# Two decoder layers on one core: FF2's units of seven products, block transposes by way of HBM, and sums behind the remainders

## The reference, cut to what matters

```python
def conv_gated_ffn(h, w_up, conv_w, conv_b, w_down):      # h 256x2048, w_up 2048x11264, w_down 5632x2048
    u = h @ w_up
    up_ = jnp.pad(u, ((0, 0), (1, 1), (0, 0)))
    u = up_[:, :-2] * conv_w[0] + up_[:, 1:-1] * conv_w[1] + up_[:, 2:] * conv_w[2] + conv_b
    gate, val = jnp.split(u, 2, axis=-1)
    return (jax.nn.silu(gate) * val) @ w_down
```

## Time and profile before

| what | value |
|---|---|
| median of 3 runs | 2124.67 us (2124.34 to 2125.66) |
| profiled execution, its own time | 2125.52 us |
| its span | 2123.4 us |
| PE busy | 2108.5 us, 99% |
| DVE busy | 1738.8 us, 82% |
| ACT busy | 1194.7 us, 56% |
| POOL busy | 80.4 us, 4% |
| HBM read | 395.80 MB, 190 GB/s over the span |

### The profile page before, as it was taken

How to read it: one execution, slowest core, us unless ns; L and a number is a source line. 1 busy time by engine, 2 the same in 40 slices (tenths; PEclk the granted TensorE clock), 3 DMA queues, 4 the chain that set the end, 5 groups by cost and what they waited for, 6 DMA issues and landing times.

```text
span 2123.4 us, 28090 instructions
## 1 busy us (share of the span) xinstructions
PE 2108.5 (99%) x9682; PEld 1753.0 (83%) x9682; DVE 1738.8 (82%) x2498; ACT 1194.7 (56%) x1562; POOL 80.4 (4%) x114
## 2 busy tenths in 40 slices
PE   9999999999999999999999999999999999999999
PEld 7897888888888888888889878888888888888887
DVE  5889977888888887979766557569999999999787
ACT  6556675555555545545466446556666666665454
POOL 1000000001000100000000042000000000000000
PEclk9999999999999999999999999999999999999999
DMA  7665355677767767566556544466666666656665
GB/s 225 197 181 169 111 181 155 214 231 231 224 208 227 237 213 242 191 215 199 173 164 173 169 115 152 148 184 187 194 191 185 199 188 194 190 184 199 210 198 178
DMA packets 219710, 404.81 MB, mean 191 GB/s; under 512 B 14335, under 2 KB 58953, under 8 KB 219371
## 3 DMA queue, kind: packets, MB, share of 16 engines
q1 hardware_dynamic: 215755, 391.13, 59.5%
q0 software_dynamic: 3696, 11.54, 1.7%
q10 hardware_dynamic: 176, 1.06, 0.1%
HBM read 395.80 MB, written 7.86 MB: 190 GB/s over the span
## 4 chain that ended last, share of the span: by engine, by line
PE 82%; DVE 11%; issue 4%; ACT 2%; DMA 0%; DVEq 0%; ACTq 0%; POOL 0%; POOLq 0%
PE ps L679 20%; PE ps L681 20%; PE ps L680 20%; PE ps L985 6%; PE ps L986 6%; PE ps L987 6%; DVE w_lo L2075 3%; DVE gate_T L2128 2%; DVE val_T L2128 1%; PE ps L717 1%; ACT w_hi L1398 1%; DVE stage L2941 1%; DVE stage L2949 1%; DVE cv L2187 1%; PE ps L741 0%
## 5 line engine op out<-in xcount | busy, mean ns | idle before, releaser
L2075 DVE TENSOR_TENSOR w_lo<-raw,w_hi 128x1024 fp32r<-128x1024 f32 (+2 forms) x701 | 837.7, 1209 | 210.5 <-ACT w_hi L1398 204.0
L1398 ACT ACTIVATE w_hi<-raw 128x1024 fp32r<-128x1024 f32 (+2 forms) x701 | 724.6, 1045 | 459.2 <-PE ps L681 348.3
L679 PE MATMUL ps<-w_hi,hT_hi 128*128 128x512 f32 (+2 forms) x1792 | 699.8, 390 | 3.0 <-DVE w_lo L2075 2.3
L681 PE MATMUL ps<-w_hi,hT_lo 128*128 128x512 f32 (+2 forms) x1792 | 690.6, 385 | 0.0
L680 PE MATMUL ps<-w_lo,hT_hi 128*128 128x512 f32 (+2 forms) x1792 | 690.3, 385 | 0.0
L679 PEld LDWEIGHTS ps<-w_hi,hT_hi 128*128 128x128 f32 x1792 | 336.6, 188 | 72.7 <-DVE w_lo L2075 6.9
L681 PEld LDWEIGHTS ps<-w_hi,hT_lo 128*128 128x128 f32 x1792 | 336.4, 188 | 63.2
L680 PEld LDWEIGHTS ps<-w_lo,hT_hi 128*128 128x128 f32 x1792 | 336.8, 188 | 59.8
L679 PE MATMUL ps<-w_hi,aT_hi 128*128 128x512 f32 x480 | 187.1, 390 | 0.8 <-DVE w_lo L2075 0.8
L681 PE MATMUL ps<-w_hi,aT_lo 128*128 128x512 f32 x480 | 186.8, 389 | 0.0
L680 PE MATMUL ps<-w_lo,aT_hi 128*128 128x512 f32 x480 | 186.7, 389 | 0.0
(11 more groups left out here) (391 smaller groups left out, 2324.0 us busy)
## 6 DMA issues: line engine op xcount, KB each, us to landing
raw<-in_w_up SPq DMA_DIRECT2D x264, 512.0 KB, 4.2
raw<-in_w_down SPq DMA_DIRECT2D x176, 512.0 KB, 4.7
raw<-in_w_gate SPq DMA_DIRECT2D x88, 512.0 KB, 3.8
raw<-in_w_in SPq DMA_DIRECT2D x80, 464.0 KB, 3.7
raw<-in_w_out SPq DMA_DIRECT2D x64, 512.0 KB, 4.0
raw<-in_w_in SPq DMA_DIRECT2D x64, 256.0 KB, 3.2
raw<-in_w_in SPq DMA_DIRECT2D x24, 448.0 KB, 3.5
turn_rows<-stage POOLq DMA_DIRECT2D x11, 512.0 KB, 5.0
```

What stands on the lines that cost most here:

```text
L679: pe.matmul(o, xh, wh, start=first, stop=False)
L681: mm = pe.matmul(o, xl, wh, start=False, stop=last)
L1398: act.activation(w_hi[:, s, :kc, :width], raw[:, s, :kc, :width], ACT.Copy).then_inc(hi_ready, 1)
L2075: dve.tensor_tensor(w_lo[:, s, :kc, :width], raw[:, s, :kc, :width], w_hi[:, s, :kc, :width].bitcast(F32), ALU.subtract).then_inc(lo_ready, 1)
```

## The change

In each of the ten loop turns of FF2 the last gate tile (pair 7) and the value tile of the same pair stand next to each other and form one unit of seven: `up_seven` on TensorE, `up_combine`, `up_combine_rest`, `up_extra` and `up_value_add` on VectorE, `up_unit_hi` on ScalarE. Its combinations `up_comb` lie where `x_sb` lies, so `x_sb` (2 MB) is stored to `x_rows` in HBM before the loop and loaded back behind it, both on GpSimd's queue.

The 16 strip transposes of each half are replaced by two block transposes, a store to HBM and four strip loads; ScalarE reads the strips (`strips2`) into `half_T` before `center2`. The gate's rows have a buffer of their own (`gate_rows`), the value's rows lie in `stage[:, 2]`. The taps of the gate stand ahead of the unit in the turn, those of the value in its last third. One turn stands ahead of the loop, written out. In the groups of w_down, `sums` stands behind the remainder of the pair's first tile instead of ahead of it, and the product of the last block is split at pair 6 of group 2.

```diff
+UP_ORDER = [(0, i) for i in range(8)] + [(1, 7)] + [(1, i) for i in range(7)]
+UP_UNIT = 7
+UNITS1 = len(FF1_UNIT) * (FB - 1)
...
+                if name == "x3":
+                    pool.dma_start(x_rows, x_sb[:].rearrange("p t n -> p (t n)")).then_inc(x_saved, 16)
+
+                    def up_strips(j, half, again):
+
+                        pool.wait_ge(turned, FB + 2 * j - 1 + half)
+                        pool.sem_inc(pool_seen)
+                        pool.dma_start(turn_rows[half], turn_out).then_inc(turn_saved, 16)
+                        pool.wait_ge(turn_saved, 16 * (FB + 2 * j - 1 + half))
+                        pool.sem_inc(pool_seen)
+                        if again and half == 0:
+                            pool.wait_ge(aT_ready, j - 1)
+                            pool.sem_inc(pool_seen)
+                        strips_back(half, stage[:, 1 + half].rearrange("p c s -> p (c s)"))
+
+                    up_strips(1, 0, False)
+                    up_strips(1, 1, False)
+                    with pool.Fori(2, FB + 1) as j:
+                        up_strips(j, 0, True)
+                        up_strips(j, 1, True)
+                    pool.wait_ge(ff_value, 2 * (FB - 1))
+                    pool.dma_start(x_sb[:].rearrange("p t n -> p (t n)"), x_rows).then_inc(x_back, 16)
...
+            def up_seven(j):
...
+                pe.wait_ge(lo_ready, c + 1 + 16 * j)
+                three(ps[:, 4, :], a11, b11, True, True)
+                three(ps[:, 0, :], a12, b21, False, True).then_inc(tile_used, 1)
+                pe.wait_ge(gemm_free[1], G_FF2 + j)
+                pe.wait_ge(lo_ready, c + 2 + 16 * j)
+                three(ps[:, 2, :], sums[3], b22, True, False).then_inc(tile_used, 1)
+                pe.wait_ge(ff_split, 2 * UNITS1 + 2 * j - 1)
+                three(ps[:, 7, :], sums[0], comb[0], True, True)
+                three(ps[:, 6, :], sums[1], comb[1], True, True).then_inc(ff_used, 1)
+                pe.wait_ge(ff_split, 2 * UNITS1 + 2 * j)
+                three(ps[:, 5, :], sums[2], comb[2], True, True)
+                three(ps[:, 1, :], a22, comb[3], False, True).then_inc(ff_used, 1)
...
+                for n in range(UP_UNIT):
+                    gemm_tile(T_FF2 + n, 16 * j, H, 2 * n, pair(0), n == 0, False)
+                up_seven(j)
+                for n in range(UP_UNIT + 2, 16):
+                    up_value_tile(n, j)
...
+            def strips2(j, half):
+
+                act.wait_ge(turn_back, 64 * (FB + 2 * j + 1 + half))
+                act.activation(by_strip(half_T[:].rearrange("p c s -> p (c s)")),
+                               stage[:, 1 + half].rearrange("p c s -> p (c s)").rearrange("p (i m a) -> p i m a", i=4, a=32),
+                               ACT.Copy).then_inc(value_turned if half else gate_turned, 1)
...
+            def up_unit_hi(j):
+
+                c = T_FF2 + UP_UNIT + 1
+                act.wait_ge(raw_landed[c % RING], landed(c, 16 * j))
+                act.wait_ge(tile_used, c - RING + 1 + 16 * j)
+                act.activation(w_hi[:, c % RING, 1, :], raw[:, c % RING, 1, :], ACT.Copy).then_inc(hi_ready, 1)
+                for i in range(2):
+                    act.wait_ge(ff_ready, 2 * UNITS1 + 2 * j - 1 + i)
+                    act.activation(up_comb_hi[:, 2 * i:2 * i + 2, :], up_comb[:, 2 * i:2 * i + 2, :], ACT.Copy).then_inc(ff_hi, 1)
+
+            def up_turn(j, after):
+
+                hi_tiles(T_FF2, 16 * j, 0, 4)
+                copy2(j - 1, 1, after)
+                hi_tiles(T_FF2, 16 * j, 4, 5)
+                strips2(j - 1, 0)
+                center2(j - 1, 0)
+                hi_tiles(T_FF2, 16 * j, 5, 7)
+                silu2(j - 1)
+                hi_tiles(T_FF2, 16 * j, 7, 8)
+                up_unit_hi(j)
+                hi_tiles(T_FF2, 16 * j, 9, 11)
+                act.wait_ge(ff_used, 2 * UNITS1 + 2 * j)
+                act.activation(up_comb[:, 0, :], ps[:, 4, :], ACT.Copy).then_inc(ff_copied, 1)
+                hi_tiles(T_FF2, 16 * j, 11, 13)
+                copy2(j, 0, True)
+                hi_tiles(T_FF2, 16 * j, 13, 14)
+                strips2(j - 1, 1)
+                center2(j - 1, 1)
+                hi_tiles(T_FF2, 16 * j, 14, 16)
+                hidden_hi(j - 1)
...
-                    if b == 0 and (q, p) in SUM_AT:
-                        sums(SUM_AT[q, p])
                     if b == 0 and p in SEVEN[q]:
                         combine(q, p)
                     if b == 1 and p in SEVEN[q]:
                         second_chunk_lo(c)
                     else:
                         split_lo(c, 0)
+                    if b == 0 and (q, p) in SUM_AT:
+                        sums(SUM_AT[q, p])
                     if (q, p, b) == (0, 6, 1):
                         turn_lo(FB - 1)
+                    if (q, p, b) == (2, 6, 1):
+                        hidden_lo(FB - 1)
...
+            def up_blocks(half):
+
+                for t in range(TOK):
+                    out = turn_out.rearrange("p (q c t a) -> p t c q a", q=4, c=4, t=TOK)[:, t]
+                    ins = dve.transpose(out, up_rows[half][:, t, :].rearrange("p (c q b) -> p c q b", c=4, q=4))
+                ins.then_inc(turned, 1)
...
+            def up_combine(j):
...
+                dve.tensor_tensor(t1, raw[:, sb_, 0, :], raw[:, sa, 0, :], ALU.subtract)
+                dve.tensor_tensor(t3, raw[:, sb_, 1, :], raw[:, sb_, 0, :], ALU.subtract).then_inc(ff_ready, 1)
+                dve.wait_ge(ff_ready, 2 * UNITS1 + 2 * j - 1)
+                dve.tensor_tensor(t2, raw[:, sb_, 1, :], t1, ALU.subtract).then_inc(ff_step, 1)
+                dve.wait_ge(ff_step, 4 * (FB - 1) + 3 * j - 2)
+                dve.tensor_tensor(t4, raw[:, sa, 1, :], t2, ALU.subtract).then_inc(ff_ready, 1)
...
+            def up_extra(j, part):
+
+                u1, u2, u3, u4 = (up_comb[:, i, :] for i in range(4))
+                if part == 0:
+                    dve.wait_ge(ff_copied, FB - 1 + j)
+                    dve.tensor_tensor(u2, ps[:, 5, :], u1, ALU.add).then_inc(ff_step, 1)
+                    dve.tensor_tensor(ps[:, 0, :], ps[:, 0, :], u1, ALU.add)
+                    dve.wait_ge(ff_step, 4 * (FB - 1) + 3 * j - 1)
+                    dve.tensor_tensor(u4, ps[:, 7, :], u2, ALU.add)
+                    dve.tensor_tensor(u3, ps[:, 6, :], u2, ALU.add).then_inc(ff_step, 1)
+                else:
+                    dve.wait_ge(ff_step, 4 * (FB - 1) + 3 * j)
+                    dve.tensor_tensor(u2, ps[:, 7, :], u3, ALU.add)
+                    dve.tensor_tensor(ps[:, 1, :], ps[:, 1, :], u3, ALU.add).then_inc(ff_added, 1)
...
+            def up_value_add(j):
+
+                dve.wait_ge(tile_used, T_FF2 + 16 + 16 * j)
+                dve.wait_ge(ff_added, FB - 1 + j)
+                dve.tensor_tensor(ps[:, 2, :], ps[:, 2, :], up_comb[:, 3, :], ALU.add)
+                dve.tensor_tensor(ps[:, 3, :], ps[:, 3, :], up_comb[:, 1, :], ALU.add).then_inc(ff_value, 1)
+                dve.wait_ge(ff_value, FB - 1 + j)
+
+            def up_turn(j, after):
+
+                lo_tiles(T_FF2, 16 * j, 0, 3)
+                if after:
+                    up_value_add(j - 1)
+                lo_tiles(T_FF2, 16 * j, 3, 5)
+                dve.wait_ge(gemm_free[1], G_FF2 + j)
+                dve.wait_ge(turn_saved, 16 * (FB + 2 * j - 1))
+                up_blocks(1)
+                lo_tiles(T_FF2, 16 * j, 5, 6)
+                taps2(j - 1, 0, (0,))
+                lo_tiles(T_FF2, 16 * j, 6, 7)
+                taps2(j - 1, 0, (1,))
+                up_combine(j)
                 lo_tiles(T_FF2, 16 * j, 7, 8)
-                taps2(j - 1, 1)
+                up_combine_rest(j)
+                lo_tiles(T_FF2, 16 * j, 9, 11)
+                up_extra(j, 0)
+                lo_tiles(T_FF2, 16 * j, 11, 12)
+                up_extra(j, 1)
+                lo_tiles(T_FF2, 16 * j, 12, 13)
+                dve.wait_ge(gemm_free[0], G_FF2 + 1 + j)
+                dve.wait_ge(turn_saved, 16 * (FB + 2 * j))
+                up_blocks(0)
+                lo_tiles(T_FF2, 16 * j, 13, 14)
+                taps2(j - 1, 1, (0,))
+                lo_tiles(T_FF2, 16 * j, 14, 15)
+                taps2(j - 1, 1, (1,))
                 product2(j - 1)
-                lo_tiles(T_FF2, 16 * j, 8, 12)
+                lo_tiles(T_FF2, 16 * j, 15, 16)
                 hidden_lo(j - 1)
-                dve.wait_ge(gemm_free[0], G_FF2 + 1 + j)
-                dve.wait_ge(aT_ready, j)
-                dve.wait_ge(ct_free, 2 * j)
-                for n in range(4):
-                    lo_tiles(T_FF2, 16 * j, 12 + n, 13 + n)
-                    ins = turn_strips(gate_T[:], raw_s, 4 * n, 4 * n + 4)
-                ins.then_inc(gate_turned, 1)
+
+            dve.wait_ge(x_saved, 16)
+            up_turn(1, False)
+            with dve.Fori(2, FB) as j:
+                up_turn(j, True)
```

(4 more changed lines are left out.)

168 lines of the change are left out of this document (101 added, 67 removed).

## The result

| | before | after |
|---|---|---|
| median, us | 2124.59 (4 runs) | 2149.55 (4 runs, 2145.68 to 2152.00) |
| profiled execution, its span | 2125.52, 2123.4 | 2145.68, 2143.9 |
| matmuls, whole page | 9682 | 9652 |

The ratio is 1.0115, interval 1.0097 to 1.0133: 25 us slower. I had forecast 2126.9 us and 2139 as the upper end. Between the profiled executions it is 20.2 us, and only those can be compared row by row. The four runs of after rose one after the other while their mean granted clock went from 1.000 to 0.998.

The account below looks back on a forecast made before the run. TensorE's matmul count was taken as the bound. On the profiled 2125.52 us, -6.8 - 3.0 + 10 x 1.0 + 10 x 0.2 + 0 + 0 = +2.2 gave 2127.7, median 2126.9 us; 8-in-10 range 2116 to 2139.

Parts of the forecast that it names:

- The products: FF2 loop: one unit in each of ten turns removes 3 matmuls per turn, saving 6.8 us.
- VectorE's lighter load: FF2 turn: VectorE's work falls by 2.3 us net, to about 39 of 42.85 us, so by sum it fits.
- The old waits: FF2 loop: the existing stalls, 0.30 us a turn, go as VectorE gets lighter, saving 3.0 us.
- The chain behind the unit: FF2, unit to last tile: TensorE waits for the last remainder, 1.0 us in each of ten turns (0.5 to 1.3).
- From there to the next unit: FF2, last tile to next unit: 0.3 us margin against 0.5 us transfer delay, 0.2 us stall a turn (0 to 1.5).
- Rival C: FF2, strips behind tile 4: gate rows return late, stalling the unit; +12 us at 6.5 us landing, 2139 us; chance 0.20.
- The range: Whole kernel: the main case's own range, 2121 to 2133 us, said to come from both bounds of the chain.
- x_sb to HBM and back: Around the FF2 loop: storing 2 MB and loading it in w_down costs 0, at most 3 us each way.
- Sums behind remainders: w_down, third group: the gap at pair 15 closes but returns at pair 16; counted 0, between -1.3 and 0.

Follow-up runs that it names:

- e3: The changed kernel, with VectorE splitting the last tile's remainder ahead of the previous block's value product; 2156.34 us, ratio 1.0145 to the kernel before.
- e6: e2 with the last tile's remainder ahead of the value's product and the hidden split behind the next turn's first tile; 2136.44 us, ratio 1.0044.
- e10: e7 with last block's product and split later in w_down, value add right behind the first tile's remainder, value rows copied one tile earlier; 2124.46 us.
- e2: The changed kernel, with gate strips returning into gate_rows in blocks 0 to 9, not waiting for the hidden split; 2134.61 us, ratio 1.0043.
- e9: The changed kernel with the two handovers moved as in e6, but gate strips still returning into stage[:, 1] behind the hidden split; 2166.79 us.
- e1: The changed kernel, with the 2 MB return of x_sb sent as eight 256 KB pieces, one after every third tile; 2146.44 us, ratio 1.0101.
- e5: The changed kernel without the unit of seven products in FF2: pair 7 multiplied plainly, transposes through HBM kept; 2126.07 us, ratio 0.9996.
- e7: e6 plus e1's spaced return of x_sb, and the last block's gate strips returning into up_comb_hi without waiting for the hidden split; 2132.62 us.
- e11: e10, with tiles 10 and 11 of w_down's second group split ahead of the last block's value strips; 2122.70 us, ratio 0.9983.
- e4: The kernel before, with only w_down's sums moved behind the tile's first remainder; 2124.81 us, ratio 0.9992.

## Why the prediction was wrong

- *The products*, -6.8 us, and VectorE's lighter load: right (30 matmuls fewer; 86% busy). So was the conclusion that order, not load, decides. *The old waits*, -3.0 us: they were five stalls of 0.5 us, -2.5.
- *The chain behind the unit*, +1.0 in each of ten turns: right, to 0.1 us. TensorE leaves the unit at 1561.20; the last remainder ends at 17.2 us after that (I had 17.15), and 1.0 + 0.1 us are lost. The step failed in one respect only: I treated the stall as a thing of its own. e3, e6 and e10 show that it belongs to a chain that closes on itself across the end of the turn.
- ***From there to the next unit*, +0.2 in each of ten turns: this is the term that failed.** It measured 1.47 us in nine. On my own scale (TensorE's leaving the unit, 1561.20, is 0) the value add came at 22.1 us (I had 21.7), the value copy at 23.4 (23.0), the rounding of tile 4 ended at 26.6 (25.2), the middle taps at 30.0 (28.2), the remainder for the unit at 40.25 (38.6). The loss arises between 23.4 and 26.6. What I had wrong there is when the gate's strips are back: I had 25.0, and the last one landed at 26.6. GpSimd's first issue came at 19.3 (I had 18.3), and the last strip took 5.67 us (I had taken 4.9, the median of all strips in the kernel before). The weights of tile 4 landed at 25.4, which pushed its rounding to 26.6 too. I had seen the two transfers fall together and put 0.5 us on it against a margin of 0.3. Both ends of that bound were mine, 0 to 1.5, and I took a value near the lower, where the margin alone should have sent me to the middle. e2 and e9 show both sides of this term.
- *Rival C* is therefore what happened: the place (ScalarE's strips behind tile 4), the cause (a return held back by the hidden split, a remainder late at the unit) and the condition (a landing beyond 5.1 us; the last strip's took 5.6 to 6.4 in these nine turns). Its price of +12 us is near what the unit cost, 13.2. Its sign, a wait of `half_T` for the DMA, is missing from the table of waits, because the rounding ahead of the read was late by nearly as much; the critical chain has it. I had given it 0.20.
- *The range.* I wrote that 2121 to 2133 came from both bounds of the chain. It did not: 1.3 and 1.5 us in ten turns give -9.8 + 13 + 15 = +18.2, and so 2142.9. Carried through, the bounds of the two terms would have reached the loop's measured loss; what then lacks is w_down.
- *x_sb to HBM and back*, 0: the way out took 8.8 us and costs nothing (TensorE has no stall in turn 1 until its last tile). The way back costs 2.4 us by the sum of stalls (3.9 by the waits alone, e1), about my upper bound of 3. *The last block in w_down* was missing from the sum: with its gate strips, product and split among the first tiles of a group that has units and sums of its own, it is most of the rest of the 7.7 us that I counted as 0. e5 shows 6.3 us of stalls there without any unit in FF2; e7, e10 and e11 take them down to 4.2. That is the second failed step. What the remaining 4.2 us wait for stays open.

  The two DMA rows behind this, from 1500 to 1850 and from 1900 to 1990 (count, KB each, us from issue to landing):

```profile
turn_rows<-stage POOLq DMA_DIRECT2D x16, 512.0 KB, 3.7
```
```profile
x_sb<-x_rows POOLq DMA_DIRECT2D x1, 2048.0 KB, 10.1
```

  512 KB (the median of 16) and 2 MB took 3.7 and 10.1 us here, beside the weight stream. By the Trainium skill ("DMA: Bandwidth & Descriptors", Anatomy of one DMA — SWDGE (gpsimd) path) it would be 3.2 and 6.8 us, as an estimate; the trace agrees within 0.5 us for the small one and not for the large one.
- *Sums behind remainders*, 0: it is -1.3 by the trace of e4, the end that I did not take. I had the gap of pair 15 come back at pair 16; e4 has none there.
- What is left between the trace's 20.2 and the medians' 25 us stays open. Over its four runs the granted clock of the changed kernel fell by 0.002, which on 2145 us would be, as an estimate, 4.3 of the 6.3 us by which they rose; I did not test what lowers it.

## What to carry to other kernels

In a loop whose engines hand work around, lay out the chain until it closes on itself, over as many turns as it takes; the time of a turn is the longest such cycle, and a stall that moves without shrinking tells that you have cut elsewhere. When a term has a margin of a few tenths against a transfer that runs beside the weight stream, work out when its last piece lands, from its own start and beside the loads in flight at that moment, and carry the upper bound into the range. And when two things end together, a table of waits names one of them at most: set the start of the reader against the landing, or read the critical chain. A block peeled off the end of a loop lands in the next stage: count its work there, against the work that stage already has.
